# Chunked recurrence in a hybrid model kernel: order of the value products and of the output projection's first half on TensorE

## The reference

```python
def step(state, inp):
    r_t, w_t, k_t, v_t, kk_t, a_t = inp
    sa = jnp.einsum('bhvk,bhk->bhv', state, -kk_t)
    state = (state * w_t[:, :, None, :]
             + sa[..., None] * (kk_t * a_t)[:, :, None, :]
             + v_t[..., None] * k_t[:, :, None, :])
    return state, jnp.einsum('bhvk,bhk->bhv', state, r_t)
...
y = ((y - mu) * lax.rsqrt(var + LN_X_EPS)).reshape(B, S, RWKV_WIDTH) * ln_x_w + ln_x_b
y = y + bonus.reshape(B, S, RWKV_WIDTH)
return y * g
...
y = jnp.concatenate([y_lru, y_rw], axis=-1).astype(x.dtype)
x = x + y @ w_out
return x + swiglu(rms_norm(x, norm_ffn), ffn_w1, ffn_w3, ffn_w2)
```

## Time and profile before

| | us |
|---|---|
| median of 3 runs | 1195.6 (1195.18 to 1196.11) |
| the profiled execution, its own time | 1193.21 |
| its span, first to last instruction | 1191.4 |
| TensorE matmul busy | 1158.4 (97%) |
| VectorE busy | 282.2 (24%) |
| ACT busy | 160.6 (13%) |
| GpSimd busy | 53.4 (4%) |

### The profile page before, as it was taken

How to read it: one execution, slowest core, us unless ns; L and a number is a source line. 1 busy time by engine, 2 the same in 40 slices (tenths; PEclk the granted TensorE clock), 3 DMA queues, 4 the chain that set the end, 5 groups by cost and what they waited for, 6 DMA issues and landing times.

```text
span 1191.4 us, 25483 instructions
## 1 busy us (share of the span) xinstructions
PE 1158.4 (97%) x11675; PEld 886.9 (74%) x11675; DVE 282.2 (24%) x683; ACT 160.6 (13%) x345; POOL 53.4 (4%) x58
## 2 busy tenths in 40 slices
PE   7999899999999999999999999999999999999995
PEld 6889878888888888874587666667768876676651
DVE  5756544000000266442210110110110111011003
ACT  4416211000000125423000000000000000000001
POOL 0012000100000000000101000010010010000010
PEclk9999799999999999999999999999999999999999
DMA  9700095475100717668999999999999999999994
GB/s 344 292 1 2 3 372 210 145 279 177 54 1 1 301 55 308 281 276 330 399 425 422 427 424 424 424 422 424 425 423 424 424 424 425 424 423 425 424 419 188
DMA packets 65410, 359.48 MB, mean 302 GB/s; under 512 B 5160, under 2 KB 14896, under 8 KB 37392
## 3 DMA queue, kind: packets, MB, share of 16 engines
q1 hardware_dynamic: 61616, 347.26, 71.7%
q0 software_dynamic: 3232, 10.36, 2.2%
q10 hardware_dynamic: 448, 0.17, 0.1%
HBM read 350.94 MB, written 6.83 MB: 300 GB/s over the span
## 4 chain that ended last, share of the span: by engine, by line
PE 93%; DMA 4%; DVE 1%; issue 0%; ACT 0%; DVEq 0%; SPq 0%
PE ps L673 93%; DMA W<-in_moe 4%; DMA W<-in_l_w_in 0%; PE ps L735 0%; DVE W L1782 0%; DVE xn L2192 0%; PE ps L1062 0%; ACT S L1606 0%; DVE W L1808 0%; DVE S L1786 0%; ACT S L1381 0%; PE ps L1100 0%; DVE W L1817 0%; DVE W L1804 0%; DVE xn L2117 0%
## 5 line engine op out<-in xcount | busy, mean ns | idle before, releaser
L673 PE MATMUL ps<-W,S 128*32 128x352 f32 (+4 forms) x6904 | 562.8, 466 | 9.6 <-DMA W<-in_moe 5.8
L673 PEld LDWEIGHTS ps<-W,S 128*32 128x32 f32 (+2 forms) x6904 | 374.3, 111 | 177.1 <-issue 69.3
L673 PE MATMUL ps<-xn,W 128*128 128x256 f32 (+1 forms) x1392 | 307.6, 380 | 0.0
L673 PEld LDWEIGHTS ps<-xn,W 128*128 128x128 f32 (+1 forms) x1392 | 263.0, 190 | 39.9 <-issue 3.3
L2132 DVE TENSOR_TENSOR S<-S,ps 128x352 f32<-128x352 f32 x44 | 22.9, 521 | 532.8 <-ACT S L1548 529.5
L673 PE MATMUL ps<-S,W 128*128 128x256 f32 (+2 forms) x648 | 140.8, 375 | 7.0 <-DMA W<-in_l_w_in 7.0
L673 PE MATMUL ps<-S 128*32 128x352 f32 (+4 forms) x1520 | 133.5, 454 | 2.9 <-DMA S<-in_moe 2.5
L673 PEld LDWEIGHTS ps<-S,W 128*128 128x128 f32 (+2 forms) x648 | 117.4, 192 | 23.5 <-issue 8.0
L673 PEld LDWEIGHTS ps<-S 128*32 128x32 f32 (+1 forms) x1520 | 81.9, 113 | 39.1 <-issue 20.9
L1548 ACT ACTIVATE S<-ps 128x352 f32<-128x352 f32 x44 | 18.7, 462 | 557.4 <-PE ps L673 554.6
L1871 DVE TENSOR_TENSOR S<-S,ps 128x256 f32<-128x256 f32 x20 | 8.4, 421 | 194.6 <-ACT S L1458 194.6
(11 more groups left out here) (296 smaller groups left out, 406.2 us busy)
## 6 DMA issues: line engine op xcount, KB each, us to landing
W<-in_moe SPq DMA_DIRECT2D x116, 1408.0 KB, 27.5
W<-in_moe SPq DMA_DIRECT2D x60, 1024.0 KB, 28.3
S<-in_moe SPq DMA_DIRECT2D x28, 1024.0 KB, 28.7
W<-in_l_ffn_w SPq DMA_DIRECT2D x12, 2048.0 KB, 10.4
S<-in_moe SPq DMA_DIRECT2D x12, 1408.0 KB
W<-in_l_ffn_w SPq DMA_DIRECT2D x6, 1536.0 KB
W<-in_l_w_in SPq DMA_DIRECT2D x4, 2048.0 KB, 20.3
W<-in_l_w_out SPq DMA_DIRECT2D x2, 4096.0 KB, 23.2
```

Of the source, the lines that this page charges most:

```text
L673: return nc.tensor.matmul(o, l, r, start=start, stop=stop, **kw)
```

## The change

The products of the values for one chunk (`values_state(c + 1)`, `values_out(c + 1)`, the latter now per chunk) stand between the u products of chunk `c` and its wait for U. Ahead of chunk 0 only those of chunk 0 are left. In the last chunk, in the same place, stand the first two output blocks of the projection's first half, with the waits for the weights and for `y_lru`. Blocks 2 and 3 stand ahead of the first statistics products, blocks 4 and 5 between the two, blocks 6 and 7 behind the second.

```diff
-            def values_out(u):
-                for c2 in range(CH):
-                    for j in range(4):
-                        for par in range(2):
-                            mm(ps[half(par), 6 + u, cols(c2, j)], Vt[half(u), c2, j, half(par)], NR[half(u), 2 * c2 + par, j, 1, :],
-                               c2 == 0 and j == 0, False, skip_group_check=True)
+            def values_out(c):
+                c2, u = divmod(c, 2)
+                for j in range(4):
+                    for par in range(2):
+                        mm(ps[half(par), 6 + u, cols(c2, j)], Vt[half(u), c2, j, half(par)], NR[half(u), 2 * c2 + par, j, 1, :],
+                           c2 == 0 and j == 0, False, skip_group_check=True)
...
             pe.wait_ge(xcp, 4 * (LV - 1))
-            for c in range(NC - 1):
-                values_state(c)
+            values_state(0)
+            values_out(0)
             for c in range(NC):
...
                     ins.then_inc(u_done, 1)
-                if c == 0:
-                    values_out(1)
+                if c < NC - 2:
+                    values_state(c + 1)
+                if c < NC - 1:
+                    values_out(c + 1)
+                if c == NC - 1:
+                    pe.wait_ge(in_wo0, 16)
+                    pe.wait_ge(y_lru, 1)
+                    project_out(wo0, range(0, 2), range(4))
                 pe.wait_ge(u_out, 2 * c + 2)
...
-                if c == 0:
-                    values_out(0)
...
-            pe.wait_ge(in_wo0, 16)
+            project_out(wo0, range(2, 4), range(4))
             pe.wait_ge(y_out, 2)
...
-            pe.wait_ge(y_lru, 1)
-            project_out(wo0, range(0, 2), range(4))
+            project_out(wo0, range(4, 6), range(4))
             pe.wait_ge(ln_sq, 1)
...
-            project_out(wo0, range(2, KD), range(4))
+            project_out(wo0, range(6, KD), range(4))
```

More of the change, by code:

```diff
@@ L847, in values_state, with project_out @@
                            c2 == 0 and j == 0, False, skip_group_check=True)
-            def values_out(u):
-                for c2 in range(CH):
-                    for j in range(4):
-                        for par in range(2):
-                            mm(ps[half(par), 6 + u, cols(c2, j)], Vt[half(u), c2, j, half(par)], NR[half(u), 2 * c2 + par, j, 1, :],
-                               c2 == 0 and j == 0, False, skip_group_check=True)
+            def values_out(c):
[4 more added lines that the diff above has]
+                           c2 == 0 and j == 0, False, skip_group_check=True)
+            def project_out(w, ds, ks):
+                for d in ds:
+                    for k in ks:
+                        ins = mm(ps[:, d // 2, (d % 2) * T:(d % 2 + 1) * T], w[:, k, d * P:(d + 1) * P],
+                                 xn[:, k, :], k == 0 and d % 2 == 0, k == KD - 1, skip_group_check=True)
+                    if d % 2 and ks[-1] == KD - 1:
+                        ins.then_inc(wo_done, 1)
+                return ins
             values_in(0)
```

## The result

| | us |
|---|---|
| kernel before, median of 15 runs | 1195.2 (1193.4 to 1197.7) |
| changed kernel, median of 15 runs | 1199.9 (1193.0 to 1202.1) |
| ratio | 1.0034, 95% interval 1.0022 to 1.0045 |
| profiled execution of the changed kernel, span | 1199.6 (before: 1191.4) |

The medians are 4.7 us apart. The ratio, which is estimated from all runs, puts the cost at 0.34%, that is 4.1 us (2.6 to 5.4 by its interval). The two profiled executions are 8.2 us apart, twice as much, and the part that the diff touches has to be told from the rest first.

The account below looks back on a forecast made before the run. TensorE, busy 97% of the span, was taken as the bound. Net new idle time +2.1 us and a clock fall +1.9 made +4.0, put on a median of 1195.6: 1199.6 us, range 1195.5 to 1203.0.

Parts of the forecast that it names:

- TensorE must stand idle for 7.72 - 3.4 = 4.3 us: Behind the second statistics products: only 16 records (3.4 us) left to cover 7.72 us until the y_rw(1) result.
- Chunks 0 to 2 at nothing: Recurrence, spread value products: chunks 0 and 1 together 0, bounds -0.3 and +0.3; chunk 2 +0.1 us.
- Rival (a): Recurrence: filled gaps hold the high clock; 1192.7 without a fall in the new idle stretch (4%), 1194.7 with one (8%).
- (d): Recurrence: clock falls earlier, near 133 us, and rises later, one more low spell: +6.8, 1202.4 us; chance 17%.
- The covered idle time less the new one, +2.1 with the low spell as before: Chunk 3 to projection's end: finished at 184.3 us instead of 182.2, net +2.1, with the clock as it was.
- the clock fall in the idle stretch: New 4.3 us idle stretch before the last 64 records: clock falls, costing 1.9 us (bounds 0 and 2.45).
- The weight loads at nothing: First-layer weight loads on SP's queue: start up to 5 us later, wanted over 30 us later, so no cost.
- Rule and row: Recurrence clock: the skill's busy-TensorE rule says no fall; the trace rows show one without gaps above 0.8 us; forecast follows rows.

Follow-up runs that it names:

- filler: 9 idle products in TensorE's idle stretch: on the changed kernel 1198.4 us, ratio 1.0030; on projection alone with idle full-array products 1194.9, ratio 1.0003 (without them 1195.4).
- The dense run: Idle full-array products in TensorE's gaps of chunks 1 to 3, against the kernel before: 1191.7 us, ratio 0.9973.

## Why the prediction was right, point by point

- The result lies 0.3 us from the forecast (1199.9 against 1199.6), slower, by the mechanism of the forecast: run alone, the projection's new place has a ratio of 1.0042 and the value products 1.0000. That it is as near as 0.3 us is partly luck: the 1199.6 stand on a median of three runs, 1195.6; against the 15 runs (1195.2) the medians moved by 4.7 us, where +4.0 was forecast.
- "TensorE must stand idle for 7.72 - 3.4 = 4.3 us": 4.16, ended by VectorE's write of xn, in every profile that has this tail and no filler. With 32 records left as cover it was 0.70 (0.9 expected).
- Chunks 0 to 2 at nothing: right in the median, but not by the step given. The spread value products go with a clock that holds in some executions (three runs of 12 at 1190), and with one that falls 2.4 us earlier, as in the profiled execution. Rival (a) and a mild form of (d) are both real, in different executions of one kernel; the prediction treated them as alternatives for the kernel. The fall came 6.8 us after the first copy and cost 0.9 us at most, where (d) had it sooner and at 2.8. The two fastest runs of the changed kernel, 1193.0 and 1193.8, lie where the first half of (a) put them (1192.7). They have no trace, but their mean granted clock of 0.994 (the other 13: 0.983 to 0.990) is that of the three shortest runs of the value products alone.
- The covered idle time less the new one, +2.1 with the low spell as before: the steps in the profile are 0.9 us later at the second statistics products (165.75 less the 1.94 of the start, 163.8 instead of 162.9). The earlier fall explains only part of it: with the projection alone the clock fell no earlier (9.4 us after the first copy, 9.2 before), and these products were still 0.4 us later than expected. In this execution the terms add up: 2.1 + 0.9 + 1.7 for the second fall = 4.7. At the high clock the net was 3.0 to 3.6 us (2.7 by the terms of the sum).
- The mis-sized term is the clock fall in the idle stretch, "I take a fall, and 1.9 us". The fall came, and took 1.4 to 1.7 us in the profiled executions. In the medians the filler that removes it is worth about 0.5 us at the high clock, and nothing that can be told within a group of the changed kernel's runs. The rest must then be larger than the +2.1 of the sum: 3.0 to 3.6 us for the wait with the clock held, and 0.5 more, are 3.5 to 4.1, which agrees with the measured 4.1 (2.6 to 5.4). So the total came out partly because two errors cancel, if the medians are to be trusted at 0.5 us. How much of the 4.1 is due to low spells inside the recurrence was not isolated.
- The weight loads at nothing: right. The first is issued at 155.47 instead of 148.19, and TensorE goes on from the projection to the feed-forward without an idle time. (The next stage's first weight load stands 6.7 us later than before, 188.91 against 182.23: the 1.9 of the start and 4.7.)
- Rule and row: the rows were right that TensorE's clock falls here without a long idle gap. The dense run adds what held it, for this kernel: full-array products in the gaps of the same loop. This goes with the Trainium skill (TensorE: Matmul & The Clock Gate, "Why this matters for your kernels") in so far as it wants TensorE busy. But the low clock of the changed kernel through 12.28 busy us of 12.50 speaks for it that what TensorE is busy with matters too. The fall after 4.2 us without any product agrees with that section's warning of idle gaps.

## What to carry to other kernels

Before independent work is pulled forward into a gap, count how much of it the later, longer wait needs as cover, and move no more than the surplus: here 2.5 us of 10.2 could go (7.7 are needed), the change moved 6.8, and 3.4 cost nothing that could be told. Size what goes into a gap by the clock that the gap has, and look at the granted clock in a loop of small products: a few full-array products in its gaps, even idle ones, were worth more (3.1 us) than any reordering (2.2 at best, and only with the clock held).

## What the runs showed of the hardware that was not expected

- Executions differ in where the clock changes: with the same code ahead of it, the first rise lay at 10.0 to 13.4 us in the twelve traces; the value products alone ran with a low spell inside the recurrence or without one, by two groups of runs 5 us apart; short spells at 539, 1143 and 1160 us stood in one trace and not in another. Spans of 1191.4 and 1199.6 hold some 3 us of this (1.5 at the start, 1.7 at 539 us).
- Small products on a quarter or half of the array did not hold the clock with TensorE busy for 2.6 of 3.3 us, and did not raise it in 12.28 busy us of 12.50; in another execution they kept it with 9.20 of 12.00. With 256, or 256 and 128, columns of full-array products in each gap it stayed at 1.00 up to 1147 us, and the runs scattered less (a standard deviation of 0.6 us instead of 1.1).
